# Down projection of the MLP: seven products instead of eight in the lower half of quarters 1 to 3 too, two products behind each up unit

## The reference

```python
def sq_relu_mlp(h, w1, w2):
    a = jax.nn.relu(h @ w1)
    return (a * a) @ w2

        x = x + sq_relu_mlp(rms_norm(x, norm_mlp[layer]), mlp_w1[layer], mlp_w2[layer])
```

## Time and profile before

| | |
|---|---|
| median of 3 runs | 2084.68 us (2084.66 to 2085.72) |
| the profiled execution, its own time | 2084.32 us |
| its span on the profile | 2082.5 us |
| PE (TensorE matmul) busy | 2074.2 us, 100% |
| DVE (VectorE) busy | 1580.3 us, 76% |
| ACT (ScalarE) busy | 1170.2 us, 56% |
| granted TensorE clock, mean | 1.00 of full speed (2.4 GHz) |
| DMA over the span | 443.28 MB, 213 GB/s |

### The profile page before, as it was taken

How to read it: one execution, slowest core, us unless ns; L and a number is a source line. 1 busy time by engine, 2 the same in 40 slices (tenths; PEclk the granted TensorE clock), 3 DMA queues, 4 the chain that set the end, 5 groups by cost and what they waited for, 6 DMA issues and landing times.

```text
span 2082.5 us, 27541 instructions
## 1 busy us (share of the span) xinstructions
PE 2074.2 (100%) x10802; PEld 1756.7 (84%) x10802; DVE 1580.3 (76%) x2105; ACT 1170.2 (56%) x1442; POOL 80.0 (4%) x74
## 2 busy tenths in 40 slices
PE   9999999999999999999999999999999999999999
PEld 8888888888888888888788888888888888888887
DVE  7798787778778877668887777656778677677777
ACT  6777475565564555665656655554445445454454
...
PEclk9999999999999999999999999999999999999999
...
GB/s 326 195 233 195 199 213 189 203 215 169 209 190 160 238 167 150 159 148 237 190 287 201 249 231 203 185 182 214 203 261 251 203 262 242 212 236 242 240 207 218
DMA packets 71746, 443.28 MB, mean 213 GB/s; under 512 B 7872, under 2 KB 14784, under 8 KB 20288
## 3 DMA queue, kind: packets, MB, share of 16 engines
q1 hardware_dynamic: 64992, 393.28, 51.4%
q0 software_dynamic: 6624, 48.24, 12.5%
...
## 4 chain that ended last, share of the span: by engine, by line
PE 89%; DVE 4%; ACT 1%; POOL 1%; issue 1%; DVEq 0%; ACTq 0%
PE bank L1230 25%; PE bank L1235 13%; PE bank L1253 12%; PE bank L1255 12%; PE bank L1257 12%; PE bank L1269 3%; PE bank L1271 3%; PE bank L1273 3%; DVE wlo L2004 2%; POOL SM L2730 1%; DVE W L2603 1%; PE bank L1360 1%; PE bank L1496 1%; PE bank L1432 1%; DVE W L2622 1%
## 5 line engine op out<-in xcount | busy, mean ns | idle before, releaser
L2004 DVE TENSOR_TENSOR wlo<-raw,whi 128x2048 fp32r<-128x2048 f32 x305 | 697.8, 2288 | 189.5 <-ACT whi L1556 157.7
L1556 ACT ACTIVATE whi<-raw 128x2048 fp32r<-128x2048 f32 x305 | 583.3, 1913 | 233.7 <-PE bank L1257 201.5
L1230 PE MATMUL bank<-A,whi 128*128 128x512 f32 x2448 | 586.8, 392 | 0.4 <-ACT whi L1556 0.4
L1230 PEld LDWEIGHTS bank<-A,whi 128*128 128x128 f32 x2448 | 451.5, 188 | 90.7 <-issue 1.9
L1235 PEld LDWEIGHTS bank<-A,wlo 128*128 128x128 f32 x2432 | 311.9, 191 | 11.8
L1235 PE MATMUL bank<-A,wlo 128*128 128x256 f32 x2432 | 315.4, 283 | 0.0
L1253 PE MATMUL bank<-whi,A2h 128*128 128x512 f32 x736 | 289.1, 393 | 0.0
L1255 PE MATMUL bank<-whi,A2l 128*128 128x512 f32 x736 | 287.0, 390 | 0.0
L1257 PE MATMUL bank<-wlo,A2h 128*128 128x512 f32 x736 | 286.8, 390 | 0.0
L1253 PE MATMUL bank<-whi,A 128*128 128x512 f32 x512 | 203.5, 397 | 0.1
L1255 PE MATMUL bank<-whi,A 128*128 128x512 f32 x512 | 200.0, 391 | 0.2
...
## 6 DMA issues: line engine op xcount, KB each, us to landing
...
```

Source lines behind the costliest of these rows:

```text
L1230: last = e.matmul(o[:, :], whi[:, s, k * P:(k + 1) * P], A1[:, k, :, :].rearrange("p h t -> p (h t)"), start=k == 0, stop=packed and k == ...
L1556: e.activation(whi[:, u % 3, :], raw_of(u), ACT.Copy).then_inc(*hi.inc((u, 3)))
L2004: e.tensor_tensor(wlo[:, u % 3, :], raw_of(u), whi[:, u % 3, :], ALU.subtract).then_inc(*lo.inc((u, 3)))
```

## The change

- Quarters 1 to 3: the lower half of the contraction is done by sevens too, in two sets `dl.s.0` and `dl.s.1` (six new sets). Of the plain units there remain the eight of quarter 0 and four of quarter 3.
- The last quarter's upper half: only the first pair of column blocks in a seven (`dp.3.0`); the second pair plainly, by `down.3.2` and `down.3.3`. In all 13 sets instead of 8, and 12 B units instead of 32.
- Order: the string `eight` puts 14 products behind 8 up units, mostly two behind one. It stands five times: `dl.1`, `dp.1`, `dl.2`, `dp.2`, `dl.3`. Quarter 0's sets keep one product behind each unit.
- Activation factors of the new sets: `low_mixed`, four sums and four low parts on VectorE and four copies on ScalarE, after `up.s.8`. Both mixes now stand over two steps.
- `d` and `f` of these sets go on in the PSUM bank of `a` (`a` is drained first), so the copy to SBUF and VectorE's adds to it (L1574, L2066) go away in the MLP, and each set has eight drains.

```diff
-    four = tag[0] in ("np", "dp")
+    four = tag[0] in ("np", "dp", "dl")
...
     for s in range(QT):
-        ups = [("A", ("up", s, i), "mlp_w1_2", (16 * s + i) * P) for i in range(0 if s else 4, 16)]
-        u += in_turn("-a-c-b-e-d-f-g", sevens("dp", "mlp_w2_2", s - 1, 1), ups) if s else ups
-        if s < QT - 1:
-            u += in_turn("-a-c-b-e-d-f-g", sevens("dp", "mlp_w2_2", s, 0), down(s, (1, 0, 2, 3)))
-    left, right = (iter(sevens("dp", "mlp_w2_2", QT - 1, p, order)) for p, order in enumerate(("acbedfg", "abcdefg")))
-    plains = iter(down(QT - 1, (1, 0, 3, 2)))
-    u += [next({"-": plains, "L": left, "R": right}[c]) for c in "-L-L-LR-L-LR-LR-LR-RRR"]
+        plains += [("A", ("up", s, i), "mlp_w1_2", (16 * s + i) * P) for i in range(0 if s else 4, 16)] + down(s)
+        sets += both("dl", s) if s else []
+        sets += both("dp", s) if s < QT - 1 else sevens("dp", "mlp_w2_2", s, 0)
+        eight = "-a-cb-ed-f-ga-cb-ed-fg"
+        if s == 0:
+            order += 12 * "-" + "-a-c-b-e-d-f-g-"
+        else:
+            order += "-a-c-b-e-d-f-g-" if s == 1 else eight
+            order += eight
+    order += "-a-cb-ed-fg"
+    u += in_turn(order, sets, plains)
...
+LEFT = ((1, 0, 2, 3),) + ((),) * (QT - 2) + ((2, 3),)
...
-        after[at["up", s, 15] + 1].append(("mix", s))
+        for part in range(2):
+            after[at["up", s, 15] + 1 + part].append(("mix", s, part))
+            if s:
+                after[at["up", s, 8] + part].append(("low mix", s, part))
...
+    if tag[0] in ("dp", "dl"):
+        return {"a": ((0, left, 1),), "b": ((1, right, 1), (0, right, 1)), "c": ((0, right, 1),), "d": ((0, right, -1),),
+                "e": ((0, left, 1),), "f": ((1, right, -1), (1, left, 1)), "g": ((1, left, 1),)}[tag[3]]
...
+                if tag[0] in ("dp", "dl"):
+                    if name in "df":
+                        w.wait_ge(*evac_v((product(u, "a" if name == "d" else "d"), 0)))
+                    opens = name in "ab" or name in "ceg" and alone(tag)
...
+            def low_mixed(s, part):
+                if part == 0:
+                    for i in range(8):
+                        w.wait_ge(*up_v("l", at["up", s, i]))
+                    a = W[:, M_H:M_H + 2048].rearrange("p (q k t c) -> p q k t c", q=2, k=4, t=NT)
+                    a11, a21, a12, a22 = (a[:, q, :, t, :] for q in range(2) for t in range(NT))
+                    e.tensor_tensor(a22, a21, a22, ALU.subtract).then_inc(*low_v.inc("1", s))
...
+                for name, high, low, x in low_parts():
+                    w.wait_ge(*low_a("h" + name, s))
+                    e.tensor_tensor(low, x, high, ALU.subtract).then_inc(*low_v.inc("l" + name, s))
```

More of the change, by code:

```diff
@@ L226, in timetable @@
     run(("r2",), at["nv", 0, 3], 7)
-    after[at["bo", 2, 0]].append(("mix", -1))
+    after[at["bo", 2, 0]] += [("mix", -1, part) for part in range(2)]
     for j in range(KVH):
@@ L232, in timetable @@
             run(("na", 0), at["nq", 0, 3] + 1, 9)
-            after[at["nv", 0, 3] + 5].append(("mix", MIX_HEADS))
+            after[at["nv", 0, 3] + 5] += [("mix", MIX_HEADS, part) for part in range(2)]
             continue
@@ L328, in unit @@
         return next(m for m, v in enumerate(units) if v[1] == units[n][1][:3] + (x,))
-    if u + 2 < len(units) and units[u + 2][1][0] in ("np", "dp"):
+    if u + 2 < len(units) and units[u + 2][1][0] in ("np", "dp", "dl"):
         then = {"a": "b", "c": "f", "b": "d", "d": "g"}.get(name(u + 2))
@@ L335, in sums @@
         yield ("acc", unit(u + 2, "b"))
-    if u + 3 < len(units) and units[u + 3][1][0] in ("np", "dp"):
+    if u + 3 < len(units) and units[u + 3][1][0] in ("np", "dp", "dl"):
         return
@@ L344, in shut @@
 def shut(tag):
-    if tag[0] == "down" and seven(tag[1], tag[2]):
+    if tag[0] == "down" and tag[1] == 0:
         return (1,) if tag[2] % 2 and tag[3] == 1 else ()
@@ L373, in block_of @@
     left, right = pair_of(tag)
+    if name in "adf":
+        return tag[:3]
+    if alone(tag):
+        return (u,)
     return {"c": (s, right, 0), "e": (s, left, 0), "g": (s, left, 1)}.get(name, (u,))
@@ L483, in last_read @@
             name = units[u][1][3] if units[u][0] == "P" else None
-            if units[u][1][0] in ("np", "dp") and name == "e":
+            if units[u][1][0] in ("np", "dp", "dl") and name == "e":
                 return u
@@ L821, in stack_kernel @@
         keep_a = Marks(sem("product_kept"), [s[1] for s in SCRIPT if s[0] == "late" and units[s[1]][0] == "P" and
[L822 removed]
+                                             units[s[1]][1][0] == "bp" and units[s[1]][1][3] == "a"])
         DRAINS, PIECE, PIECES, EMPTIED = {}, {}, {}, {}
@@ L900, in parts_of @@
             high, low = (mixr[:, i, 0:1024].rearrange("p (k t c) -> p k t c", k=4, t=NT) for i in range(2))
+            yield ("4", *(mixr[:, i, 1024:1536].rearrange("p (k c) -> p k c", k=4) for i in range(2)), a[:, 1, :, 0, :])
             if s == MIX_HEADS:
@@ L906, in parts_of, with low_parts @@
                 yield "1", A1h[:, 0:4, 0:P], A1l[:, 0:4, 0:P], a[:, 1, :, 1, :]
+            yield "2", high[:, :, 0, :], low[:, :, 0, :], a[:, 0, :, 0, :]
             yield "3", high[:, :, 1, :], low[:, :, 1, :], a[:, 0, :, 1, :]
+        def low_parts():
+            a = W[:, M_H:M_H + 2048].rearrange("p (q k t c) -> p q k t c", q=2, k=4, t=NT)
+            high, low = (mixr[:, i, 0:1024].rearrange("p (k t c) -> p k t c", k=4, t=NT) for i in range(2))
+            yield ("4", *(mixr[:, i, 1024:1536].rearrange("p (k c) -> p k c", k=4) for i in range(2)), a[:, 1, :, 0, :])
+            yield "1", A2h[:, 0:4, P:T], A2l[:, 0:4, P:T], a[:, 1, :, 1, :]
             yield "2", high[:, :, 0, :], low[:, :, 0, :], a[:, 0, :, 0, :]
-            yield ("4", *(mixr[:, i, 1024:1536].rearrange("p (k c) -> p k c", k=4) for i in range(2)), a[:, 1, :, 0, :])
+            yield "3", high[:, :, 1, :], low[:, :, 1, :], a[:, 0, :, 1, :]
         hb = [W[:, M_HB + t * 512:M_HB + (t + 1) * 512] for t in range(NT)]
@@ L1268, in product_block @@
                     wh, wl = (x[:, u % 3, k * 512:(k + 1) * 512] for x in (whi, wlo))
-                    e.matmul(o, h, wh, start=name in ("a", "b", "d", "f") and k == 0, stop=False)
+                    e.matmul(o, h, wh, start=opens and k == 0, stop=False, skip_group_check=goes_on)
                     w.wait_ge(*low_made)
-                    e.matmul(o, low, wh, start=False, stop=False)
+                    e.matmul(o, low, wh, start=False, stop=False, skip_group_check=goes_on)
                     w.wait_ge(*lo((u, 3)))
-                    last = e.matmul(o, h, wl, start=False, stop=k == 3)
+                    last = e.matmul(o, h, wl, start=False, stop=k == 3, skip_group_check=goes_on)
                 last.then_inc(*mm.inc((u, 0)))
@@ L1298, in factor @@
                 which = {"b": "1", "c": "4", "d": "2", "f": "3"}[name]
+                if kind == "dl":
+                    return h, low, (low_a("h" + which, s), low_v("l" + which, s))
                 return h, low, (mix_a("h" + which, mix_round(s)), mix_v("l" + which, mix_round(s)))
@@ L2718, in vector_program @@
                     "halve": halve, "total": total, "quarter": quarter, "x3": x3, "aff": affine, "r2": r2, "att": att, "gate": gate,
-                    "nk": na_keys, "open": opened, "na": na, "add": add, "mix": mixed, "upb": upb}
+                    "nk": na_keys, "open": opened, "na": na, "add": add, "mix": mixed, "low mix": low_mixed, "upb": upb}
             for step in SCRIPT:
```

119 lines of the change are left out of this document (72 added, 47 removed).

## The result

| | before | after |
|---|---|---|
| median of the runs | 2085.1 us (2084.7 to 2085.7, 5 runs) | 2144.1 us (2143.8 to 2149.2, 5 runs) |
| ratio | | 1.0289, 95% interval 1.0274 to 1.0304 |
| span of the profiled execution | 2082.5 us | 2142.0 us |

The changed kernel is 59 us slower. The forecast was 2150, with 2110 to 2180 as the range. It lies inside, 6 us from the middle, so the sign and the size were right. What has to be shown is whether the reason was.

A forecast was written before the change was run, and what follows sets the result against it. TensorE was taken to bound the kernel, but after the change to wait for chains of accumulating weight DMAs: 2084.3 - 12.4 of matmuls + 78.5 of new waits = 2150 us, range 2110 to 2180.

The forecast's parts named there:

- TensorE's work, -12.4 us: On TensorE 20 B units go (108.8 us) and 35 products come (95.2 plus 1.2 us): -12.4 us.
- VectorE fits at 94% and costs nothing: In one `eight`, VectorE's 77.9 us of work fits in TensorE's 83.1 us.
- 3 + 1.5 us for them: Waits at the mixes ahead of `a`: 3 us in all between sets, 1.5 us at the last set.
- A link is 13.5 us, and 11.0 is too short: From one chain product's `lo` to the next's takes 13.5 us; TensorE's distance is 11.0, so it waits about 2.4.
- The sum of the waits, 78.5: New TensorE waits: 67 us over five `eight`s, less 2, plus 3 for mixes, plus 10.5 in the last set.
- I take half of the 3.4 us, 1.7: `d`'s DMA queued behind `f`'s lands 1.7 us later, so `d` in the first set costs 4.2 us.
- `b` 2.3, `d` 2.5, `g` 2.4: Waits in us at the three chain products in the second set of each `eight`.
- 2.4 + 4.2 + 2.4 + 1.5 = 10.5: Waits in the last set, between B units: all its links short and a mix right ahead, 10.5 us.
- No link is too long: Rival: accumulating DMAs land within 6.2 us, no link waits, 2072 or up to 2078 us; chance 0.06.
- The DMA engines are the bound: Rival: 85.2 us of transfers per `eight` against TensorE's 83.1 set the time, 2084 us, no change; chance 0.03.
- The crowd: Rival: accumulating DMAs share with plain loads, landings 10 us, link 14.8, whole 2189 us; chance above 2180 is 0.05.
- what the forecast said the profile would show: TensorE's busy time falls; some 75 us idle in some 27 waits; ScalarE waits 5 to 6 us; `eight`s about 96.

The follow-up runs named there:

- the kernel with plain tiles: The changed kernel with the second tiles of `b`, `d`, `f`, `g` in the MLP loaded plainly, without adding: 2080.2 us, ratio 0.9977.
- the two-chain order: The changed kernel with both sets of each `eight` side by side and `c`'s tiles asked for later: 2081.0 us, ratio 0.9985.
- the one with `f` behind: The changed kernel with GpSimd issuing `f`'s accumulating DMA behind `d`'s instead of ahead of it: 2179.6 us, ratio 1.0461.

## Why the prediction was right

**TensorE's work, -12.4 us: right.** Where nothing waits an `eight` takes 83.08 us against the 83.1 summed, and the kernel with plain tiles comes within 6 to 8 us of the full gain.

**VectorE fits at 94% and costs nothing: right for the `eight`s.** It is 77% busy, and 31 us less work for it gained nothing. In the two-chain order the same work takes it 74 to 75 us of 83 and fits without a wait. It is not nothing where the mixes stand. The forecast had 3 + 1.5 us for them; the mix ahead of the last set alone cost 3.9, 1.3 at `a` and 2.6 at the plain unit behind it:

```profile
2102.15 0.50 PE L1291 MATMUL bank<-wlo,A2h 128*128 128x512 f32 x1 [2.26 <-DVE wlo L2056]
```

**A link is 13.5 us, and 11.0 is too short: right, and shown three ways.** From `lo` to `lo` the links of the change took 12.8 to 16.1 us, 13.8 in the middle (only the very first, with a lead and no hurry, took 16.9). With a landing of 5.1 us the waits go; with 1.08 us more per link 27 us come; with 19.3 us of distance or more neither the adding DMA nor 3 us of delay costs an `eight` anything.

**The sum of the waits, 78.5: too large by 6.6 (71.9 measured), and its parts are less good than the sum.** The excess of each product over its pitch (2.72, or 2.80 on `mixr`), in us over all five `eight`s:

| | forecast | measured |
|---|---|---|
| first set `b`, `d`, `g` | 10 + 21 + 0 - 2 = 29 | 9.3 + 15.4 + 0 = 24.7 |
| second set `b`, `d`, `g` | 11.5 + 12.5 + 12 = 36 | 4.3 + 22.1 + 7.2 = 33.6 |
| mixes (`a`), up units | 3 | 3.6 |
| last set, its products | 10.5 | 3.8 |
| last set, ahead of `wlo` of two plain units | | 3.8 |
| ahead of the MLP | | 2.1 |
| not placed | | 0.3 |

These include the matmuls at half clock, up to 15.3 us that the forecast did not have at all. Whether they come on top is open: a link runs on VectorE, GpSimd, the DMA and ScalarE, so a slow matmul between two waits may fill time in which TensorE would have waited anyway. If they do come on top, the waits alone are some 55 us (71.9 - 15.3 - 2.1), the forecast had priced them over 20 too high, and it was luck that the clock, which it left out, made up for most of that. If they don't, the price was some 9 us too high (78.5 against 71.9 - 2.1). The steps that were off:

- "I take half of the 3.4 us, 1.7: `d` in the first set costs [...] 4.2": it cost 3.1 on average. Its DMA, issued 4.8 to 5.7 us behind `f`'s, landed after 8.5 to 9.0 us in four first sets of the `eight`s and after 11.2 in one, where 10 to 11 were expected. Two edits that take `f` away from in front of `d` did not lower the cost (2.9 and 4.1). The effect exists (a landing of 11.8 and 14.0 us for `d` in the last sets of two kernels, 12.0 for `g` in the one with `f` behind), but it hits whatever overlaps `f`.
- "`b` 2.3, `d` 2.5, `g` 2.4" in the second set: where `b` did not wait (twice of five), `d` paid 5.8 and 4.9 us, in the other three 3.8 on average. The lead is handed along the chain, so the sum of a set can be forecast and a single product's share can't.
- "2.4 + 4.2 + 2.4 + 1.5 = 10.5" for the last set: it cost 7.6, and otherwise than forecast. The links were 2.6 of it (`d` 1.9, `g` 0.7) instead of 9.0, the mix 3.9 instead of 1.5, and 1.2 went to a plain unit whose plain load was late (ScalarE's `hi` waited 2.1 us for it). In the two-chain kernel, where TensorE arrives there without having waited, `d` alone cost 6.5. In the change the waits of `g` and `a` ahead of it may have given its chain a lead; that was not tried.

**The rivals.** *No link is too long* needs a landing of 6.2 us, and none that adds was under 7.9 in the change, or under 7.8 in any run. *The DMA engines are the bound*: its 85.2 us of transfers in an `eight` were too high, since an `eight` of 83.08 us left the engines 4 to 9% free. *The crowd*: landings were 8.8 in the middle, not 10. Of what the forecast said the profile would show, TensorE's busy time did not fall but rose by 12.1 us, by the half clock and the rows next to waits; 27 late products were 25; 75 us of idle time of TensorE were 55.7, since part of each wait is booked as busy; waits of ScalarE of 5 to 6 us were 5.0; `eight`s of 96 us were 92 to 102, from last product to last product.
